# Moving one 64-byte tile: activation tiles 64 and 32 bytes off the weights modulo 512

## What is computed

```python
merged = jax.nn.sigmoid(ga) * a_out + jax.nn.sigmoid(gb) * c_out
x = x + jnp.einsum('btd,de->bte', merged, w_out[l])
h2 = rmsnorm_2(x, norm_ffn[l])
g, up = jnp.split(jnp.einsum('btd,df->btf', h2, w_gate_up[l]), 2, axis=-1)
x = x + jnp.einsum('btf,fd->btd', jax.nn.silu(g) * up, w_down[l])
```

## Time and profile before

| | |
|---|---|
| median of 3 runs | 2253.84 us (2253.67 to 2254.68) |
| the profiled execution | 2255.32 us |
| its span | 2253.4 us |
| TensorE busy | 2226.5 us, 99% |
| VectorE, ScalarE, GpSimd busy | 1254.4, 937.7, 235.2 us |
| granted clock, mean | 0.999 of 2.4 GHz |

### The profile page before, as it was taken

The page is one execution under the profiler, slowest core; times in us unless marked ns, Lnnn a source line. Parts: engine busy times, 40 slices in busy tenths (PEclk is TensorE's granted clock), DMA queues, the critical chain, the costliest instruction groups (busy, mean ns, idle before and its releaser), DMA issues.

```text
span 2253.4 us, 29343 instructions
## 1 busy us (share of the span) xinstructions
PE 2226.5 (99%) x11388; PEld 1823.5 (81%) x11388; DVE 1254.4 (56%) x1842; ACT 937.7 (42%) x1507; POOL 235.2 (10%) x218
## 2 busy tenths in 40 slices
PE   9999999999999999999999999999999999999999
PEld 7887888898888898886678888888886768888887
DVE  6468656445444225998664444333989664544433
ACT  5545454354333225226954333222333963433322
POOL 3000032011000001022031000001003122000001
PEclk9999999999999999999999999999999999999999
DMA  5221033122222232221122222222321122332232
GB/s 214 106 77 57 20 120 126 55 75 97 107 95 93 95 112 75 105 76 56 57 75 85 102 93 97 107 94 105 112 75 57 38 76 75 115 108 93 93 112 74
DMA packets 29909, 203.20 MB, mean 90 GB/s; under 512 B 3440, under 2 KB 4080, under 8 KB 6128
## 3 DMA queue, kind: packets, MB, share of 16 engines
q1 hardware_dynamic: 28512, 197.34, 24.4%
q10 hardware_dynamic: 1296, 4.46, 0.5%
HBM read 199.69 MB, written 2.10 MB: 90 GB/s over the span
## 4 chain that ended last, share of the span: by engine, by line
PE 87%; DVE 8%; ACT 2%; issue 2%; POOL 1%; DMA 0%; ACTq 0%; POOLq 0%; DVEq 0%
PE bank L415 25%; PE bank L417 25%; PE bank L416 25%; DVE cy L2352 3%; PE bank L999 1%; PE bank L2130 1%; PE bank L2117 1%; PE bank L2107 1%; DVE w_lo L301 1%; PE bank L970 1%; POOL acc L324 1%; PE bank L987 1%; PE bank L2007 1%; PE bank L1590 1%; PE bank L1567 1%
## 5 line engine op out<-in xcount | busy, mean ns | idle before, releaser
L415 PE MATMUL bank<-x_hi,w_hi 128*128 128x512 f32 (+1 forms) x2032 | 790.7, 389 | 6.3 <-DVE w_lo L301 2.7
L417 PE MATMUL bank<-x_hi,w_lo 128*128 128x512 f32 (+1 forms) x2032 | 775.5, 382 | 0.0
L416 PE MATMUL bank<-x_lo,w_hi 128*128 128x512 f32 (+1 forms) x2032 | 774.6, 381 | 0.0
L301 DVE TENSOR_TENSOR w_lo<-w_raw,w_hi 128x2048 fp32r<-128x2048 f32 x167 | 386.5, 2315 | 398.7 <-ACT w_hi L297 398.7
L297 ACT ACTIVATE w_hi<-w_raw 128x2048 fp32r<-128x2048 f32 x167 | 319.7, 1916 | 578.3 <-PE bank L417 576.4
L415 PEld LDWEIGHTS bank<-x_hi,w_hi 128*128 128x128 f32 x2032 | 382.4, 188 | 84.2 <-issue 6.8
L417 PEld LDWEIGHTS bank<-x_hi,w_lo 128*128 128x128 f32 x2032 | 382.1, 188 | 74.7
L416 PEld LDWEIGHTS bank<-x_lo,w_hi 128*128 128x128 f32 x2032 | 382.7, 188 | 72.5 <-issue 2.9
L415 PE MATMUL bank<-f_hi,w_hi 128*128 128x512 f32 (+1 forms) x572 | 213.5, 373 | 0.0
L416 PE MATMUL bank<-f_lo,w_hi 128*128 128x512 f32 (+1 forms) x572 | 213.3, 373 | 0.0
L417 PE MATMUL bank<-f_hi,w_lo 128*128 128x512 f32 (+1 forms) x572 | 213.3, 373 | 0.0
(11 more groups left out here) (354 smaller groups left out, 2652.1 us busy)
## 6 DMA issues: line engine op xcount, KB each, us to landing
w_raw<-w_d SPq DMA_DIRECT2D x184, 1024.0 KB, 4.8
out_d<-h SPq DMA_DIRECT2D x4, 512.0 KB, 6.3
h<-x_d ACTq DMA_DIRECT2D x3, 512.0 KB, 9.2
tab<-rope_d ACTq DMA_DIRECT2D x2, 640.0 KB, 3.8
memT<-mem_d ACTq DMA_DIRECT2D x1, 1024.0 KB, 4.7
w_raw<-w_d SPq DMA_DIRECT2D x2, 256.0 KB, 4.0
h<-x_d ACTq DMA_DIRECT2D x2, 256.0 KB, 5.8
w_raw<-w_d SPq DMA_DIRECT2D x1, 512.0 KB, 6.6
```

The lines of the kernel that those rows point to most:

```text
L301: dve.tensor_tensor(w_lo[:, u.slot, :], w_raw[:, u.slot, :], w_hi[:, u.slot, :], ALU.subtract).then_inc(lo_ready, 1)
L415: pe.matmul(dst, wh[:, k, cols], hi[:, kx_, at:at + width], start=start, stop=False)
L416: pe.matmul(dst, wh[:, k, cols], lo[:, kx_, at:at + width], start=False, stop=False)
L417: return pe.matmul(dst, wl[:, k, cols], hi[:, kx_, at:at + width], start=False, stop=stop)
```

## The change

`picks` is placed behind `sq` in place of ahead of `rcol`, and the line that moves the cursor ahead of `cy` is removed. No instruction is added, removed or put elsewhere; addresses alone differ.

```diff
         eps_c = place("eps_c", [P, 3])
-        picks = place("picks", [P, QB * QB])
         rcol, rcol_mem = place("rcol", [P, QB]), place("rcol_mem", [P, 2])
...
         sq = place("sq", [P, 2, T])
+        picks = place("picks", [P, QB * QB])
         scope = where[0]
...
         la = place("la", [P, 4, PAD + T], F32, a)
-        a[0] += (scope - a[0]) % (P * 4)
         cy_at = a[0]
         cy = place("cy", [P, 4, T], F32, a)
```

## The result

The changed kernel takes 2257.97 us, the kernel before 2254.43 us in the same runs (medians of 20 each): ratio 1.0016, 95% interval 1.001 to 1.0022, slower by 3.5 us. The profiled span went from 2253.4 to 2256.7 us. The prediction said 2262.0 us, +8.2, so the direction and the place (TensorE's streams) were right and the sum was more than twice too large.

The account below looks back on a forecast made before the run. The prediction took TensorE's start-to-start matmul distance as the bound; +6.7 us for `f`, +1.5 merged and 0 for 256 columns made +8.2, span 2261.6 and median 2262.0 us, range 2250 to 2276.

Parts of the forecast that it names:

- What bounds the kernel: TensorE, busy 99% of the span: matmul starts 226.7 ns apart, 13.3 ns above streaming 512 columns, hidden by nothing.
- Sensitive to addresses: Whether TensorE's start-to-start distance responds to addresses: settled 226.7 ns, unsettled 4.4 above; groups with operands apart modulo 512 don't settle.
- The two unsettled groups: Gate projection, 231.3 ns, and compression, 116.8 ns: stationary tiles elsewhere modulo 512 than the streamed ones, at offsets changing by chunk.
- the prediction's own last sign: In the profile after, the prediction is wrong if `f` keeps its pace or settles on a value no unsettled row shows.
- lost settling: Likeliest case: moved products in TensorE's down projections no longer settle and run at 231 ns; chance 0.42.
- no effect: Rival: settling depends on timing after an interruption, not addresses; 2253.8 us, 2251 to 2256; chance 0.34.
- The price, +4.6 ns for every moved product of 512 columns: Gate's 231.3 ns minus settled 226.7: +6.7 us for 1452 products of `f`, +1.5 for about 320 merged ones.
- Convolution, nothing, at most 0.9 us: 192 products of `c_hi` and `c_lo`, in short runs between attention jobs, hardly settled already: nothing, at most 0.9 us.
- 256 columns, taken as 0 between -1.9 and +1.9: 648 moved products of 256 columns, between the compression's -3.0 ns and +3 ns each (-1.9 to +1.9 us), taken as 0.
- Steadily dearer: Rival: streams collide for good at a constant offset, 240 ns, +24 us, 2278 us; chance 0.12 for +12 to +30.
- Faster: Rival: the 13.3 ns are a collision that shrinks 64 bytes apart in down projections; -5.5 us at 3 ns saved; chance 0.12.
- The rule of two independent read ports: Skill rule cited against the prediction: loading next weights takes no bandwidth from the running TensorE matmul, so the sum is 0.

Follow-up runs that it names:

- e1: The change with the line that moves the cursor ahead of `cy` kept, so merged tiles lie 64 off too; 2254.99 us against the kernel before's 2255.04, ratio 1.0003.
- e2: The kernel before with 32 added in the cursor line ahead of `cy`, so only `cy` and what follows lie 32 off; 2257.05 against 2255.04 us, ratio 1.0007.
- the sweep: Four kernels with other offsets from the weights, by padding ahead of `h` and the scope or moving the weights; 2284.41, 2286.99, 2294.9 and 2295.8 us.
- e4: Against the kernel before, weights placed behind everything, every streamed tile 64 bytes before them modulo 512 (448 off); 2294.55 against 2255.04 us, ratio 1.0175.
- e7: Against the kernel before, padded so unit input lies 32, feed-forward and memory 96, merged tiles 128 bytes off the weights; 2294.9 us, one run.

## Why the prediction came out as it did

- *What bounds the kernel*: right. The whole difference is in start-to-start distances of TensorE; nothing hid it, and no other engine's time moved by more than 0.2 us.
- *Sensitive to addresses*: right, and now shown and not argued: `e1`, `e2` and the sweep change nothing but places. The two unsettled groups pointed the right way. But what they showed isn't what happened to `f`: `f` settles on a cycle of three, with a mean of 228.9 ns that no unsettled row shows. By the prediction's own last sign its mechanism, lost settling, is wrong for `f`; that the direction came out right is in part luck. Nor do 64 and 32 being multiples of 16 bytes make them free, as the case for no effect had it.
- *The price, +4.6 ns for every moved product of 512 columns*: the step that failed, as a term mis-sized. For `f`, 1452 x 4.6 = +6.7 us was predicted, 3.3 measured (2.3 ns each). The nearest row was a group whose offset changes with each chunk, and by what turned out to count it is an average: steps of 96 bytes over eight chunks pass through all eight multiples of 32 modulo 256, wherever the group lies. The mean of the table's values for these eight (160 taken from its pair) is 232.0 ns, an estimate, and the gate has 231.3. In the changed kernel the gate's own tiles moved by 64 bytes: its distances changed one by one (the first five from 227, 234, 229, 232, 231 to 238, 228, 227, 230, 225 ns) and its mean stayed at 231.3. A constant offset of 64 is cheaper than that average, and cheaper than 32, 96, 128 or 192 (233 ns). One price for 64 and 32 was wrong: merged +1.5 us predicted, +2.0 measured.
- *Convolution, nothing, at most 0.9 us*: 0.5 measured.
- *256 columns, taken as 0 between -1.9 and +1.9*: -0.5 for `f` and -1.7 for the memory, -2.2 together, below the bound. The row of the compression had the sign right (116.8 against 120) and I set it aside for its 62 columns.
- *Other engines and DMAs, nothing*: right. That everything else in the scope stays aligned with itself was not quite so, since `ident` lies outside it; its transposes cost the same (109.0 ns). With the measured sizes the sum is 3.3 + 2.0 + 0.5 - 0.5 - 1.7 = +3.6 us; the runs say +3.5, with an interval from 2.3 to 5.0. Of what the forecast had too much, 3.4 us are the price of `f` and 2.2 the narrow products; the merged and the convolution terms were too small by 0.5 each.
- *The rivals*: no effect is excluded by the interval. Steadily dearer is the kind of thing that happened, at 2.3 ns for `f` and 6.6 for the merged products in place of that rival's 13.3; 12 us and up is what 32 bytes or 192 cost where `x` moves too. Faster does happen, at 256 columns alone, and too seldom here. That it isn't width-independent was in no rival.
- *The rule of two independent read ports* (the Trainium skill, TensorE: Matmul & The Clock Gate, Step-by-step: what each phase is for): by it no placement could matter. The runs disagree, with up to 3% of the distance (226.7 to 234.3 ns) set by the offset between the streamed and the stationary tile; the measurement decides. What in the chip makes the offset count, these runs don't show.

## What to carry to other kernels

Where a long stream of matmuls in this format reloads its stationary tile every time, the distance from start to start is the number to read, and it depends on where the streamed tile lies from the stationary one modulo 256 bytes: at 512 columns, of thirteen offsets tried, 0 and 256 were cheapest and 64 and 320 the next. Such an offset can cost 1.7% of a kernel (`e4`), and a pad of 32 bytes ahead of `h` cost the products of `x` 30 us by their paired distances (`e7`, one run); place the tiles that are multiplied with each other a multiple of 256 bytes apart. This is shown for fp32r products with 128 x 128 stationary tiles in this one program; float32 matmuls in it showed nothing of the kind. A price taken from another width or from an offset that moves isn't a price, only a bound.

## What the runs showed that was not expected

- At 512 columns the period is 256 bytes, half of the 512 that a stationary tile takes of each partition.
- A stream settles on a repeating pattern: at offset 0 on one distance of 226.7 ns, mostly after nine matmuls where `x` follows other work; at 64 on three of 232, 226 and 229, after three. With high and low part at different offsets it runs between 224 and 241 ns.
- At 256 columns the order is turned round: 0 is among the dearest (120 ns), 113.3 the cheapest, and the same offset can give 113.3 or 117.8.
- A stretch of 3.4 us at 1.2 GHz lands in different places of the same work or not at all, the changed kernel's in the middle of products that follow one another without idle time; in it the products of 256 columns take their columns' time and no more.
- A group whose offset steps through all multiples of 32, as the gate, hides the effect: its mean doesn't move when the group does.
